# Weighted sums of fetched rows issued in pairs in place of rows of four, in a hybrid encoder layer with expert retrieval

## What is computed

```python
v1, i1 = lax.top_k(s1, 16)          # per token and head, over 128 keys
v2, i2 = lax.top_k(s2, 16)
cand = v1[..., :, None] + v2[..., None, :]
...
g = jax.nn.softmax(top_s, axis=-1)
u = jnp.take(expert_u, idx, axis=0)
act = jax.nn.gelu(jnp.einsum("thkd,td->thk", u, hb))
vv = jnp.take(expert_v, idx, axis=0)
return jnp.einsum("thk,thkd->td", g * act, vv)
```

## Time and profile before

| | us |
|---|---|
| median of 3 runs | 2109.81 (2107.15 to 2113.86) |
| the profiled execution | 2108.62 |
| its span | 2106.8 |
| TensorE busy (matmul) | 1687.1 |
| VectorE busy | 1220.3 |
| ScalarE busy | 708.0 |
| GpSimd busy | 599.9 |

### The profile page before, as it was taken

The page is one execution under the profiler, slowest core; times in us unless marked ns, Lnnn a source line. Parts: engine busy times, 40 slices in busy tenths (PEclk is TensorE's granted clock), DMA queues, the critical chain, the costliest instruction groups (busy, mean ns, idle before and its releaser), DMA issues.

```text
span 2106.8 us, 22263 instructions
## 1 busy us (share of the span) xinstructions
PE 1687.1 (80%) x7420; PEld 765.7 (36%) x7420; DVE 1220.3 (58%) x3172; ACT 708.0 (34%) x2204; POOL 599.9 (28%) x584
## 2 busy tenths in 40 slices
PE   5899998599787997989957777767777776877776
PEld 2775897445453444444421221112121121211111
DVE  2434216766764563458756777767777765554554
ACT  2225202123772322243223333343333333333332
POOL 0000000033223332322324443435443443333331
PEclk7999999799778999999989999999999999999999
DMA  9455632299769897978949999999999999999996
GB/s 399 157 198 210 245 120 79 84 418 415 303 241 352 354 396 323 402 299 354 291 173 422 422 421 421 421 421 416 422 421 422 421 421 393 422 421 421 422 421 277
DMA packets 102467, 718.50 MB, mean 341 GB/s; under 512 B 13584, under 2 KB 13584, under 8 KB 15696
## 3 DMA queue, kind: packets, MB, share of 16 engines
q0 software_dynamic: 82944, 604.02, 70.4%
q1 hardware_dynamic: 18544, 110.69, 13.4%
q10 hardware_dynamic: 864, 2.36, 0.3%
HBM read 712.30 MB, written 4.73 MB: 340 GB/s over the span
## 4 chain that ended last, share of the span: by engine, by line
DMA 43%; PE 34%; DVE 12%; issue 5%; ACT 4%; POOL 1%; SPq 0%; DVEq 0%; POOLq 0%; ACTq 0%
DMA ring<-in_expert_uv_dram,uidx 41%; PE ps L797 8%; PE ps L540 7%; PE ps L659 6%; DVE ring L1437 4%; PE ps L680 3%; PE ps L665 2%; PE ps L720 1%; POOL ring L415 1%; PE ps L536 1%; PE ps L512 1%; DMA ring<-in_wpack_dram 1%; PE ps L570 1%; PE ps L603 1%; ACT wsel L1044 1%
## 5 line engine op out<-in xcount | busy, mean ns | idle before, releaser
L797 PE MATMUL ps<-ring,wdiag 128*32 128x512 f32 x2304 | 863.3, 632 | 246.7 <-ACT wdiag L1049 227.8
L1437 DVE CUSTOM_DVE_ANT_0 ring<-ring,mA 128x1024 f32<-128x1024 f32 x576 | 702.4, 1224 | 529.7 <-DMA ring<-in_expert_uv_dram,uidx 525.4
L415 POOL DMA_INDIRECT ring<-in_expert_uv_dram,uidx x576 | 598.6, 1039 | 1426.2 <-PE ps L797 990.2
L797 PEld LDWEIGHTS ps<-ring,wdiag 128*32 128x32 f32 x2304 | 173.3, 113 | 882.1 <-ACT wdiag L1049 542.4
L1042 ACT ACTIVATE gel<-act_in 128x1 f32<-128x1 f32 x576 | 116.8, 203 | 891.0 <-DVE act_in L1437 890.4
L1049 ACT ACTIVATE wdiag<-repeat,wsel 128x32 f32<-128x32 f32 x576 | 185.1, 321 | 18.9
L1044 ACT ACTIVATE wsel<-gel,gsel 128x1 f32<-128x1 f32 x576 | 169.6, 295 | 18.7
L540 PE MATMUL ps<-hB,ring 128*128 128x384 f32 x320 | 108.8, 492 | 0.0
L720 PE MATMUL ps<-hB,ring 128*128 128x384 f32 x256 | 89.3, 501 | 8.5 <-issue 8.5
L659 PE MATMUL ps<-hB,ring 128*128 128x384 f32 x256 | 91.3, 513 | 5.5 <-DVE kv L1278 5.5
L540 PEld LDWEIGHTS ps<-hB,ring 128*128 128x128 f32 x320 | 59.1, 190 | 42.1 <-issue 5.5
(11 more groups left out here) (233 smaller groups left out, 1599.1 us busy)
## 6 DMA issues: line engine op xcount, KB each, us to landing
ring<-in_wpack_dram SPq DMA_DIRECT2D x96, 1024.0 KB, 8.7
ring<-in_expert_uv_dram,uidx POOLq DMA_INDIRECT x576, 20.4
xB<-in_x_b_dram SPq DMA_DIRECT2D x2, 1536.0 KB, 18.4
o_y_p<-mA ACTq DMA_DIRECT2D x16, 128.0 KB, 5.4
bias<-in_bias_dram SPq DMA_DIRECT2D x1, 1024.0 KB, 29.8
o_v_p<-kv SPq DMA_DIRECT2D x4, 256.0 KB, 7.5
o_k_p<-xB SPq DMA_DIRECT2D x4, 256.0 KB, 13.7
xB<-in_keysT_dram SPq DMA_DIRECT2D x1, 1024.0 KB, 7.7
```

What stands on the lines that cost most here:

```text
L415: nc.gpsimd.indirect_dma_start(out=ring[:, slot, :], out_offset=None, in_=ins["expert_uv"], in_offset=bass.IndirectOffsetOnAxis(ap=uidx[:, ...
L797: mm = nc.tensor.matmul(pY[c * GT:(c + 1) * GT, half, :], wdiag[:, n % NDIAG, :], ring[:, ROW[n][0], D + half * 512:D + (half + 1) * 512], ...
L1437: nc.vector.tensor_tensor_reduce(r, r, h2n[:, g % 2, :], 1.0, 0.0, ALU.mult, ALU.add, act_in[:, g % 2, j:j + 1]).then_inc(s["dot"], 1)
```

## The change

TensorE's `gather(n)` issues the sums of two fetches at every odd n from 3 on, where it issued the sums of four at n = 5, 9, 13 and so on. Sum k is issued at step k + 3 or k + 2, where it was at step k + 5 to k + 2. Tiles, buffers, the strip of each sum, the order of the sums among each other and all other engines' programs stay.

```diff
                 def gather(n):
-                    if n >= REP and n % REP == 1:
-                        for k in range(n - 1 - REP, n - 1):
-                            fold(k)
+                    if n >= 3 and n % 2:
+                        fold(n - 3)
+                        fold(n - 2)
                     m = n - 2
                     g, j = m // GT, m % GT
```

## The result

The changed kernel takes 2128.0 us (median of 4 runs, 2125.5 to 2130.5) where the kernel before takes 2110.4 (2107.2 to 2113.9): a ratio of 1.0083, 95% interval 1.006 to 1.0106, slower by 17.6 us. Forecast were 41 us. The profiled execution of the changed kernel took 2130.5 us, that of the kernel before 2108.6, and their spans differ by 21.9 us.

The account below looks back on a forecast made before the run. DMA bound the late stretch; work given to TensorE tended to lengthen the early one. Terms 55.5 + 15 + 3 - 12 - 12 - 5 - 3.5 = +41 us gave 2151 us, range 2118 to 2188 us.

Parts of the forecast that it names:

- Blocks in attention: Attention: 16 pairs at 3.53 us each, 56.5 us, where 8 rows took 28.22 us.
- rival 3: Attention: filled idle time may raise the granted clock; 2131 us, at the far end about 2110 us; chance 0.16.
- Blocks elsewhere: Early stretch outside attention: 73 pairs at 1.91 us, 139.4 us; going in and out of 45 added blocks, 9 us.
- Late sums go where the fetch was their cause: Early stretch: 35 us of busy time and 15.9 us idle from late sums vanish where fetches caused them.
- New waits in key retrieval: Key retrieval: pairs wait for dots behind VectorE's top-k, +15 us, bounds 0 and 27 us.
- Slots: Two fetches run in the hole at `place(2)`, -5 us; slots freed ahead of `place(3)` and `place(4)`, -3.5 us.
- Rival 1: Early stretch: slots set the pace, so even fetches shrink TensorE's idle time; faster, 2092 us; chance 0.09.
- Rival 2: Early stretch: pairs are late as rows were, from ScalarE and VectorE order; 2202 us; chance 0.13.

Follow-up runs that it names:

- pairs_slots_as_rows: Against the changed kernel: pairs on TensorE kept, but GpSimd waits for a whole row's four sums before fetching into its slots; 2157.0 us, ratio 1.0208 to the kernel before.
- single_sums: Against the changed kernel: every sum in a block of its own, at each step from 3 on, in place of pairs; 2232.2 us, ratio 1.0542 to the kernel before.
- pairs_attention: Against the kernel before: pairs only from step 33 to 69 (attention), rows of four elsewhere; 2097.6 us, ratio 0.9919.
- rows_pair_at_place: Against the kernel before: rows of four kept, but the next two sums also issued at steps 115, 179, 307 and 435, ahead of `place` steps; 2105.7 us, ratio 0.9963.

## Why the prediction was right or wrong

**Right: the direction and most of the mechanism.** TensorE is the bound of the early stretch outside attention, a block costs the same whatever it holds, and nothing follows in the late stretch but what the slots give. Outside attention there are 36 blocks more, which at 2 us are 72. Fewer sums run late (behind the others of their block, for want of their weights) and idle time is filled, so that the kernel gets 38.6 us longer there up to `place(2)`.

**Wrong: the size, by more than half.** The sum gave +41 us, the median moved by 17.6, the profiled span by 21.9. By its terms:

- *Blocks in attention* is the term that was mis-sized. I priced 16 pairs at the 3.53 us of a row at that stretch's clock, 56.5 us, and left the dense work as long as it was. With what goes in and out of 8 blocks, less 12 us of idle time filled and 2 of late sums, my terms make attention grow by 28.3 + 1.6 - 12 - 2 = 16 us; it shrank by 10. In the changed kernel line 797 is busy for 48.2 us in attention, in place of 32.2 in the same stretch before: +16.0 for my +29.9. The other work, at no change in my sum, shrinks from 69.7 to 60.6 us. The idle time falls by 17.0 us (31.8 to 14.8) for my 14. The price was read at a clock that the change itself raises, from 0.77 to 0.89, 34 us less at the lower level. Of these 26 us, 9 are what earlier slots bring in attention, by `pairs_slots_as_rows`; the other 17 are there without them. The 26 us are more than the whole miss of 19 to 23; the other stretches together went 8 us the other way, less 2 by which the first sum starts sooner. This was rival 3, at 0.16 and priced at -20 us. Its far end is added up wrongly: with 25 + 15 us from the clock and the other 20 us of idle time it would be about 2090 us, where I wrote 2110.
- *Blocks elsewhere*, by stretch. In the projection my terms make 8 blocks at 2.1 us, less 12.5 us of lateness and plus 3, about +7; measured +12.2, with a first sum that starts 2.2 us sooner. In merge and output projection they make 18 blocks at 2.1, less 18.5 of lateness (13.2 of busy, 5.3 of idle time) and 8 at `place(1)`, +11; measured +14.3, as TensorE's wait at `place(1)` fell by 6.1 us. `single_sums` and the timelines confirm the 2.0 us. The 0.2 us for going in and out doesn't follow from the two stretches that I gave for it (10.59 and 7.91 us make 2.7 us for 8 matmuls and leave nothing over); it does from 2.85 and 5.43 us.
- *Late sums go where the fetch was their cause*: right for merge and output projection, where one of 35 pairs has its second sum 1.4 us late and nothing is waited for at the sums. Over the stretch, sums take 221.4 us of busy and idle time, above the 195 to 215 that I had named, since key retrieval and the second norm keep late sums. `pairs_slots_as_rows` costs 26 us, so slots were a cause.
- *New waits in key retrieval*, +15 us: seen, in another form. The idle time at the sums stays (6.3 us in place of 6.8), and 18 pairs are busy for 45.8 us where 1.91 each would make 34.4: second sums that come late and run by themselves for 1.9 us. Together that is 17.7 us. The stretch grew by 11.0 us, where my terms gave about 16; the scores are waited for for 1.7 us in place of 6.3, which I hadn't foreseen.
- *Slots*: at `place(2)` two fetches start in the hole, as said, and the dots from fetch 180 to 185 take 14.5 us in place of 19.9, -5.4 us for my -5. At `place(4)` the share of the DMA engines stays at 0.98 and above where it fell to 0.79, yet the dots from 185 to the last take 983.6 us in place of 982.7. So of the -3.5 us nothing is left at the end; where it goes isn't settled. The late stretch is 4.4 us shorter, for my 8.5.

One number agrees by luck. All sums together are busy for 72.1 us more, and my 56.5 + 139.4 + 9 - 133.5 is 71. In attention they take 14 us less than that, elsewhere 15 us more, where late second sums that run alone stand for the waits that I had put down as idle time. The idle time of the stretch fell by 40 us where my terms made 22.

Rival 1 (faster) was wrong for this kernel, but its two parts are real: `pairs_attention` and `rows_pair_at_place` are what it would have been without the blocks in the dense stretches. Rival 2 (the lateness comes from the order of ScalarE and VectorE and stays everywhere, 2202 us) is ruled out by the result; in key retrieval alone the lateness stays.

Open: why the clock rises. Over the ten profiles a TensorE with less idle time in attention goes with a higher clock, by sums or by repeated scores, though not strictly (0.92 with 21.9 us of idle time, 0.89 with 14.8); how the chip decides it, no run here shows. Nor is the clock's part of the 17 us parted from that of the idle time that blocks fill: with repeated scores the clock rose and the stretch got no shorter.

## What to carry to other kernels

When small blocks of work are put between dense work on one engine, look at what a block costs rather than what its parts cost: four sums on four column strips took 1.94 us, one took 1.90, so a batch split in two costs twice as much, and earlier slots are all that it brings. Splitting pays only where the engine idles anyway (here attention) or where something is about to block behind it (here `place`), and a kernel that splits only there beats both forms. A price read in a stretch at a lowered clock must not be multiplied by more work, since more work can raise that clock, as it did here from 0.77 to 0.89.

## What was not expected of the hardware

Added matmuls were nearly free in a stretch with idle gaps: 96 repeated score matmuls, 15.7 us of busy time, cost the kernel 4 us (interval -0.6 to 9.5), at a granted clock of 0.84 in place of 0.74 to 0.77; and with 9 added blocks of sums the same stretch was 6 to 17 us shorter, 9 us of it from earlier slots. A mean clock of 0.77 there meant 61 us at 1.2 GHz in 134 us.
